# An opening on x^T laid out by the host, with the first two weight blocks in float32 for both token tiles

## The reference

```python
x = x + 0.5 * swiglu(rms_norm(x, ffn1_norm[l]), ffn1_wg[l], ffn1_wu[l], ffn1_wd[l])
x = x + hybrid_mixer(rms_norm(x, mix_norm[l]), positions, rel_bias, w_in[l], ...)
x = x + 0.5 * swiglu(rms_norm(x, ffn2_norm[l]), ffn2_wg[l], ffn2_wu[l], ffn2_wd[l])
```

## Time and profile before

| | us |
|---|---|
| median of 3 runs | 855.93 |
| the profiled execution | 856.22 |
| its span (first to last record) | 853.9 |
| TensorE busy | 846.0 |
| VectorE busy | 638.0 |
| ScalarE busy | 528.9 |

### The profile page before, as it was taken

How to read it: one execution, slowest core, us unless ns; L and a number is a source line. 1 busy time by engine, 2 the same in 40 slices (tenths; PEclk the granted TensorE clock), 3 DMA queues, 4 the chain that set the end, 5 groups by cost and what they waited for, 6 DMA issues and landing times.

```text
span 853.9 us, 11996 instructions
## 1 busy us (share of the span) xinstructions
PE 846.0 (99%) x4759; PEld 735.7 (86%) x4759; DVE 638.0 (75%) x809; ACT 528.9 (62%) x762; POOL 59.1 (7%) x65
## 2 busy tenths in 40 slices
PE   9999999999999999999999999999999999999997
PEld 8988888888889988888888887888888898888885
DVE  5999999987698656665466558858777777877873
ACT  6677777756575544653454356548676676776772
POOL 0022222310000000000000000100000001000001
PEclk9999999999999999999999999999999999999999
DMA  8976566554644655566546645577565664953501
GB/s 269 346 243 199 186 197 197 189 162 154 212 148 131 215 179 192 172 238 231 171 153 225 214 148 168 197 231 236 192 222 174 213 192 150 294 173 110 187 1 50
DMA packets 123847, 161.43 MB, mean 189 GB/s; under 512 B 3976, under 2 KB 111248, under 8 KB 123664
## 3 DMA queue, kind: packets, MB, share of 16 engines
q1 hardware_dynamic: 122176, 153.85, 54.9%
q0 software_dynamic: 1312, 6.29, 2.2%
q10 hardware_dynamic: 304, 0.53, 0.2%
HBM read 159.61 MB, written 1.05 MB: 188 GB/s over the span
## 4 chain that ended last, share of the span: by engine, by line
PE 97%; DVE 1%; ACT 1%; issue 0%; POOL 0%; POOLq 0%; DVEq 0%
PE pAcc L451 23%; PE pG L385 9%; PE pU L385 9%; PE pAcc L385 7%; PE pG L391 5%; PE pR L385 5%; PE pU L391 5%; PE pM L385 4%; PE pAcc L391 3%; PE pR L391 2%; PE pM L391 2%; PE pAcc L429 2%; PE pAcc L430 2%; PE pAcc L431 2%; PE pG L529 1%; PE pM L429 1%
## 5 line engine op out<-in xcount | busy, mean ns | idle before, releaser
L326 DVE TENSOR_TENSOR lo<-raw,hi 128x2048 fp32r<-128x2048 f32 x131 | 298.3, 2287 | 53.7 <-ACT hi L321 53.7
L321 ACT ACTIVATE hi<-raw 128x2048 fp32r<-128x2048 f32 x140 | 266.0, 1910 | 13.8 <-DMA raw<-in_ffn_wd 4.1
L385 PE MATMUL pG<-xT,hi 128*128 128x512 f32 x336 | 83.4, 390 | 0.0
L385 PE MATMUL pU<-xT,hi 128*128 128x512 f32 x320 | 80.0, 392 | 0.0
L451 PE MATMUL pAcc<-hi,h_hi 128*128 128x512 f32 x240 | 74.5, 392 | 0.0
L385 PEld LDWEIGHTS pG<-xT,hi 128*128 128x128 f32 x336 | 62.8, 188 | 13.6 <-issue 0.7
L451 PE MATMUL pAcc<-lo,h_hi 128*128 128x512 f32 x240 | 74.0, 389 | 0.0
L451 PE MATMUL pAcc<-hi,h_lo 128*128 128x512 f32 x240 | 73.9, 389 | 0.0
L1166 ACT ACTIVATE h_hi<-h 128x512 fp32r<-128x512 f32 x28 | 17.7, 633 | 80.3 <-PE pAcc L451 74.5
L385 PEld LDWEIGHTS pU<-xT,hi 128*128 128x128 f32 x320 | 58.0, 189 | 10.6
L1702 DVE TENSOR_TENSOR h_lo<-h,h_hi 128x512 fp32r<-128x512 f32 x28 | 19.2, 688 | 46.0 <-ACT h_hi L1166 45.9
(11 more groups left out here) (522 smaller groups left out, 1662.8 us busy)
## 6 DMA issues: line engine op xcount, KB each, us to landing
raw<-in_a_w_in SPq DMA_DIRECT2D x24, 1024.0 KB, 5.3
raw<-in_ffn_wd SPq DMA_DIRECT2D x22, 1024.0 KB, 5.6
raw<-in_ffn_wg SPq DMA_DIRECT2D x21, 1024.0 KB, 5.4
raw<-in_ffn_wu SPq DMA_DIRECT2D x21, 1024.0 KB, 6.2
raw<-in_w_in SPq DMA_DIRECT2D x16, 1024.0 KB, 5.5
raw<-in_a_w_out SPq DMA_DIRECT2D x8, 1024.0 KB, 5.1
raw<-in_w_kv SPq DMA_DIRECT2D x8, 1024.0 KB, 5.5
raw<-in_b_w_qz SPq DMA_DIRECT2D x8, 1024.0 KB, 5.4
```

What stands on the lines that cost most here:

```text
L321: act.activation(HI[n % NHL][:, :], RAW[n % NRAW][:, :], ACT.Copy).then_inc(S["hi"], 1)
L326: dve.tensor_tensor(LO[n % NHL][:, :], RAW[n % NRAW][:, :], HI[n % NHL][:, :].bitcast(f32), ALU.subtract).then_inc(S["lo"], 1)
L385: end = pe.matmul(v3(bank[:, :], 2), wh[:, k, w], x4[:, :, k, :], start=start and k == 0, stop=not start and k == KD - 1, skip_group_check ...
```

## The change

The host lays out x^T beside x: for each token tile, 128 features on the partitions, and 8 chunks of them by 128 tokens along the row. The kernel loads its four pieces on SyncE's queue, the first two ahead of block 0, the others behind it. The norm vector is alone and first on ScalarE's queue. No x is transposed; TensorE's list has six idle multiplies, the vector's transpose, three more idle multiplies, and then float32 products only: blocks 0 and 1 for both tiles. Block 1 is never split. Block 2 is split in halves instead (`hi_first`, `lo_first`).

The squares are now of x^T, so the sum over features is made in two steps: VectorE adds over the 8 chunks (`sum_first`), TensorE over the 128 partitions, by a product with a column of 1/1024 (`mean_square`). The rows of x, which the residual needs at the end of the first swiglu, are loaded later, by one DMA of 1 MB ahead of block 8's. Block 4's load waits until block 0 is multiplied, block 5's until block 1 is; before, both waited for block 0, and for the splits of blocks 0 and 1. The tensors for the bias are laid out by the host for all 128 partitions, in two loads instead of four, behind block 3.

```diff
         def load_block(sp, n):
-            if n >= NRAW:
+            if n in (NRAW, NRAW + 1):
+                sp.wait_ge(S["used"], n - NRAW + 1)
+            elif n > NRAW:
                 sp.wait_ge(S["lo"], n - NRAW + 1)
-            if n in (NRAW, NRAW + 1):
-                sp.wait_ge(S["used"], 1)
...
+        def load_x_t(engine, b):
+            c = slice(b * 512, (b + 1) * 512)
+            engine.dma_start(XRAW[:, c], T["x_t"][:, c]).then_inc(S[f"x_in{b}"], 16)
...
+        def load_x(sp):
+            sp.wait_ge(S["x_sum"], 2)
+            sp.dma_start(v3(X[:, :], NT), T["x"][0].rearrange("(t p) c -> p t c", p=P)).then_inc(S["x_rows"], 16)
...
+        def mean_square(pe, t):
+            pe.wait_ge(S["x_sum"], t + 1)
+            pe.matmul(VAR[t], SSQ[:, t * P:(t + 1) * P], MEAN, start=True, stop=True).then_inc(S["x_var"], 1)
+
         def pe_start(pe):
-            busy(pe, 7)
-            x_transposes(pe, 0, 0)
-            pe.wait_ge(S["gain0"], 16)
+            busy(pe, 6)
+            pe.wait_ge(S["gain_first"], 16)
             pe.transpose(ACC[1][:, 0:KD], G8, IDENT[0:KD, 0:KD]).then_inc(S["gc_ps"], 1)
-            x_transposes(pe, 0, 1)
+            busy(pe, 3)
             pe.wait_ge(S["xf0"], 1)
             pe.wait_ge(S["first0"], 16)
             first_block(pe, 0, G, 0, range(0, 4))
             pe.wait_ge(S["xf1"], 1)
             pe.wait_ge(full[0], LANDED[0])
-            first_block(pe, 0, G, 0, range(4, 6))
+            first_block(pe, 0, G, 0, range(4, KD))
+            mean_square(pe, 0)
+            pe.wait_ge(S["xf2"], 1)
+            first_block(pe, 0, G, 1, range(0, 4))
             power_row(pe, 0)
-            first_block(pe, 0, G, 0, range(6, KD))
-            x_transposes(pe, 1, 0)
-            x_transposes(pe, 1, 1)
+            pe.wait_ge(S["xf3"], 1)
+            first_block(pe, 0, G, 1, range(4, 6))
+            mean_square(pe, 1)
+            first_block(pe, 0, G, 1, range(6, KD)).then_inc(S["used"], 1)
             pe.wait_ge(S["first1"], 16)
-            first_block(pe, 1, U, 0, range(0, 4))
+            first_block(pe, 1, U, 0, range(0, 2))
             power_row(pe, 1)
+            first_block(pe, 1, U, 0, range(2, 4))
             pe.wait_ge(full[1], LANDED[1])
             first_block(pe, 1, U, 0, range(4, KD))
-            pe.wait_ge(S["xf2"], 1)
-            pe.wait_ge(S["xf3"], 1)
-            first_block(pe, 0, G, 1, range(0, KD)).then_inc(S["used"], 1)
-            pe.wait_ge(S["lo"], 2)
-            pe.wait_ge(S["xt_lo"], 3)
-            to_tokens(pe, 1, U, XT, (1,), half_way=4).then_inc(S["used"], 1)
+            first_block(pe, 1, U, 1, range(0, KD)).then_inc(S["used"], 1)
+            pe.wait_ge(S["xt_lo"], 4)
...
         def xt_first(dve, b):
-            dve.wait_ge(S["xt_ps"], b + 1)
-            dve.tensor_tensor(xf(b), v3(XBANK[b][:, :], 4), fbc(GC[:, 4 * (b % 2):4 * (b % 2) + 4], P),
+            dve.wait_ge(S[f"x_in{b}"], 16)
+            dve.tensor_tensor(xf(b), x_raw(b), fbc(GC[:, 4 * (b % 2):4 * (b % 2) + 4], P),
                               ALU.mult).then_inc(S[f"xf{b}"], 1)
+        def square_first(act, b):
+            act.wait_ge(S[f"x_in{b}"], 16)
+            half = slice(4 * (b % 2), 4 * (b % 2) + 4)
+            act.activation(squares(b // 2).rearrange("p c k -> p k c")[:, half, :], x_raw(b), ACT.Square).then_inc(S["ssq"], 1)
+
+        def sum_first(dve, t):
+            dve.wait_ge(S["ssq"], 2 * t + 2)
+            dve.tensor_reduce(SSQ[:, t * P:(t + 1) * P], squares(t), AX.X, ALU.add).then_inc(S["x_sum"], 1)
...
# VectorE, second factor of the first h
-                        dve.tensor_tensor(H[:, BC:512], U[:, BC:512], SA[:, BC:512], ALU.mult).then_inc(S["h"], 1)
+                        k = RS_COL["norm", 0, 1][0]
+                        dve.scalar_tensor_tensor(out=H[:, BC:512], in0=U[:, BC:512], scalar=ST[:, k:k + 1], in1=SA[:, BC:512],
+                                                 op0=ALU.mult, op1=ALU.mult).then_inc(S["h"], 1)
...
# SyncE
-            load_x(sp, 0, 0)
+            load_x_t(sp, 0)
+            load_x_t(sp, 1)
             load_half(sp, 0, 0)
             load_half(sp, 0, 1)
-            load_x(sp, 1, 0)
-            load_x(sp, 1, 1)
+            load_x_t(sp, 2)
+            load_x_t(sp, 3)
             load_half(sp, 1, 0)
             load_half(sp, 1, 1)
             load_block(sp, 2)
-            sp.dma_start(POS[:, 0:TOK], T["positions"][0].partition_broadcast(P),
-                         allow_slow_non_contiguous=True).then_inc(S["bias_pos"], 16)
...
             load_block(sp, 3)
+            sp.dma_start(POS[:, 0:TOK + NT], T["bias_positions"]).then_inc(S["bias_pos"], 16)
+            sp.dma_start(TABLES[:, 4 * NSTEP:], T["bias_tables"]).then_inc(S["bias_pos"], 16)
             for n in range(LEAD + 1, NB):
                 b = BLOCKS[n - LEAD]
-                if b == ("ffn1", "gate", 3):
+                if b == ("ffn1", "gate", 2):
+                    load_x(sp)
+                elif b == ("ffn1", "gate", 3):
...
# ScalarE
-            load_x(act, 0, 1)
             load_gain_first(act)
             act.wait_ge(S["half"], 1)
             warm(act, ACT.Square)
-            for t in range(NT):
-                for c in range(2):
-                    act.wait_ge(S[f"x_in{t}{c}"], 16)
-                    square(act, 0, t, c)
+            for b in range(4):
+                square_first(act, b)
+            warm(act, ACT.Silu)
             xt_hi_first(act, 0)
             xt_hi_first(act, 1)
-            hi_half(act, 0)
-            hi_half(act, 1)
-            warm(act, ACT.Silu)
             xt_hi_first(act, 2)
             xt_hi_first(act, 3)
-            hi(act, 2)
+            hi_first(act, 0)
+            hi_first(act, 1)
...
# VectorE
             xt_first(dve, 0)
             xt_first(dve, 1)
-            variance(dve, 0, 0)
+            sum_first(dve, 0)
+            xt_first(dve, 2)
+            xt_first(dve, 3)
+            variance_first(dve, 0)
+            sum_first(dve, 1)
             norm_first(dve, 0)
             norm_first(dve, 1)
-            variance(dve, 0, 1)
-            xt_first(dve, 2)
-            xt_first(dve, 3)
+            variance_first(dve, 1)
             xt_lo_first(dve, 0)
             xt_lo_first(dve, 1)
             norm_first(dve, 2)
             norm_first(dve, 3)
-            lo_of_half(dve, 0)
-            lo_of_half(dve, 1)
             xt_lo_first(dve, 2)
             xt_lo_first(dve, 3)
-            lo(dve, 2)
+            lo_first(dve, 0)
+            lo_first(dve, 1)
```

More of the change, by code:

```diff
@@ L57 @@
 NRAW, NHL = 4, 4
+UNSPLIT = 2
 LEAD = 3
@@ L100 @@
     "hi": "hi parts of weight blocks", "lo": "lo parts of weight blocks", "used": "weight blocks multiplied",
-    "x_in00": "x of token tile 0 loaded, its first half", "x_in01": "its second half",
-    "x_in10": "x of token tile 1 loaded, its first half", "x_in11": "its second half",
+    "x_in0": "x^T of token tile 0 loaded, its first half", "x_in1": "its second half",
+    "x_in2": "x^T of token tile 1 loaded, its first half", "x_in3": "its second half",
+    "x_sum": "squares of a token tile summed over the chunks of features",
+    "x_var": "and over the features of a chunk", "x_rows": "x loaded", "mean": "1 / D",
     "first0": "first half of weight block 0 loaded", "first1": "first half of weight block 1 loaded",
@@ L105 @@
     "xf2": "that of token tile 1, first half", "xf3": "its second half",
-    "gc_ps": "first gain by features in a bank", "gc": "and in SBUF", "rb": "powers of the first norm along columns",
-    "hi_first": "hi part of the first half of block 1",
+    "gain_first": "first gain loaded", "hi_first": "hi part of the first half of block 2", "gc_ps": "first gain by features in a bank", "gc": "and in SBUF", "rb": "powers of the first norm along columns",
     "const_in": "lambda vectors, subln gain and DFT matrices loaded",
@@ L296, in load_half, with hi_first, lo_first @@
                 full[n] if half else S[f"first{n}"], 16)
-        def hi_half(act, half):
-            act.wait_ge(*((full[1], LANDED[1]) if half else (S["first1"], 16)))
+        def hi_first(act, half):
+            if not half:
+                act.wait_ge(full[UNSPLIT], LANDED[UNSPLIT])
             c = slice(half * KD * BC // 2, (half + 1) * KD * BC // 2)
-            op = act.activation(HI[1][:, c], RAW[1][:, c], ACT.Copy)
-            if half:
[L305 to L314, removed]
+            op = act.activation(HI[UNSPLIT][:, c], RAW[UNSPLIT][:, c], ACT.Copy)
+            op.then_inc(*((S["hi"], UNSPLIT + 1) if half else (S["hi_first"], 1)))
+        def lo_first(dve, half):
+            dve.wait_ge(*((S["hi"], UNSPLIT + 1) if half else (S["hi_first"], 1)))
+            c = slice(half * KD * BC // 2, (half + 1) * KD * BC // 2)
+            op = dve.tensor_tensor(LO[UNSPLIT][:, c], RAW[UNSPLIT][:, c], HI[UNSPLIT][:, c].bitcast(f32), ALU.subtract)
+            if half:
+                op.then_inc(S["lo"], UNSPLIT + 1)
```

(25 more changed lines are left out.)

35 lines of the change are left out of this document (16 added, 19 removed).

## The result

The changed kernel takes 856.92 us (median of 22 runs, 855.96 to 860.09), the kernel before 855.92 (22 runs beside them, 855.41 to 856.27). The ratio is 1.0018, 95% interval 1.0012 to 1.0024. The forecast was 855.55, the range 854.7 to 856.5. By the medians the change makes the kernel slower by 1.0 us, by the means, which the highest times pull up, by 1.5 us (857.41 against 855.89). Its times scatter five times as far: 12 runs lie between 855.96 and 856.93 (the lower group), nine between 857.50 and 858.86 and one at 860.09 (the upper group). 0.2% would be 1.71 us; the ratio is just within it, its interval reaches beyond.

A forecast was written before the change was run, and what follows sets the result against it. TensorE was taken to bound the kernel. Start -0.94, low clock +0.43, transposes -0.88, block 1 +0.57 and feature sums +0.44 gave -0.38 us, so 855.93 became 855.55; range 854.7 to 856.5.

The forecast's parts named there:

- Which bound: Whole kernel: TensorE bounds it, busy 846.0 of 853.9 us; only shortening its list or starting it sooner gains time.
- The same bytes stand before it now, so I leave it there: Opening loads: block 0's first half still lands at 5.96 us, with 512 KB of x ahead of it.
- bound 6.44: Block 0's first-half landing: later bound, for one more DMA issued ahead on SyncE's queue, 0.48 us.
- Rival 3: Opening: weights or VectorE's chain to block 2 are the wait; 855.9 to 856.4 us; chance 0.18 shared with another rival.
- the prediction's own signs: Changed trace: wrong if start moves under 0.5, spacing halves before 6.5 or after 8.3, or TensorE waits between 21 and 60.
- The start at 6.04: First real product on TensorE: starts at 6.04 instead of 6.98 us, 0.94 gained, 0.5 at the worst bound.
- The level of the clock: TensorE's opening: clock still rises at about 7.4, so three records instead of one run low, 0.43 us lost.
- rival 2: TensorE's opening: a standstill delays the clock's rise, 0.213 us per further low record, up to 858.3 us; chance 0.12.
- The sums on TensorE: Two sums over features by one-column products: 0.22 us each, 0.44 for both, bounds 0.22 and 0.86.
- The chain to block 2: VectorE's work to block 2: last half ends at 20.5, needed at 21.35, so 0.85 us are left.
- The loads: Later weights and rows of x: block 4 issued at about 14, block 5 at 21.4; cost taken as nothing.
- The sum: Opening's TensorE total: -0.38 us, ending at 21.35, passed whole to the kernel's end.

The follow-up runs named there:

- f4_vec_late: Changed kernel with x^T's second piece moved to the head of ScalarE's queue, the norm vector behind it; median 855.26 us.
- e2_gap: Changed kernel without the three idle multiplies behind the norm vector's transpose; median 858.39 us.
- e0_after: The changed kernel run once more, with no edit; median 858.62 us.
- g2_late_gap: f4_vec_late without the three idle multiplies behind the norm vector's transpose; median 856.79 us.
- e1_fill: Changed kernel with six idle multiplies instead of three behind the norm vector's transpose; median 856.75 us.
- g4_weights_first: Changed kernel with block 0's first half first on SyncE's queue, x^T's first piece then the vector on ScalarE's, two idle multiplies behind the transpose; median 856.93 us.
- h2_best: f4_vec_late with four idle multiplies instead of three behind the norm vector's transpose; median 855.87 us.
- h1_vec_waits: Changed kernel with the norm vector's load issued only after x^T's first piece has landed, behind ScalarE's table load; median 861.70 us.

## Why the prediction was wrong

- **Which bound, and that the opening's end passes to the kernel's end whole:** right. The span less the opening's end is 832.2 to 832.3 in every trace.
- **"The same bytes stand before it now, so I leave it there" (block 0 at 5.96, bound 6.44):** this step failed. The measured landings are 6.92 to 8.1. The bytes are the same, but before, one of the pieces of x was issued on the second queue at the first moment, and I counted the move as 0.48 us of issue time only. With that piece back at the head of the second queue (f4_vec_late) the block lands at 5.76 and the median is 855.26. Rival 3 named the weights as the wait, but took the 6.44 of the bound for the worst landing. By the prediction's own signs, a start that moves by less than 0.5, it was wrong: the first product moved from 6.98 to 7.06.
- **The start at 6.04:** all but the weights was as said: vector transposed at 4.65, its copy started at 4.69, the first half of x^T multiplied by 5.5. The idle multiplies ended at 6.05.
- **The level of the clock, three low records, no gap in TensorE's work:** the gap was there, by the failed step. In e2_gap its cost is rival 2's, a late rise, with the place and the price per record named there (0.213): 3.0 us. In e0_after (1.6 us) it is another, which I hadn't named: the clock had risen and was put back. And I took the standstill as 0.44 at most and gave the rival 0.12; about half of the executions are of the upper group, by one or the other. The sentence of the Trainium skill on the rise (TensorE: Matmul & The Clock Gate, What's actually happening), that it comes at another point from run to run, is borne out: the first product ran wholly at the upper level in after, whereas before's first record ran low, and in two executions of the same kernel the last six idle records took 1.47 (after) and 0.94 (e0_after). I turned it down on three runs; 22 runs of before lie 0.86 us apart.
- **The sums on TensorE:** a sum over features took 0.12, not 0.22, but each group of products behind it took 0.1 more than priced. From the end of the first product to the end of the opening I had 11.05 (10.3 to 21.35), measured 11.03.
- **The chain to block 2:** forecast 20.5, measured 18.70 + 2.36 = 21.06, TensorE takes it at 21.4 to 21.8. It held, with no wait.
- **The loads:** block 4 was issued at 14.80, block 5 at 21.82; no TensorE wait is seen from 21.8 to 190.
- **The sum:** in the trace of after the end is 21.78 instead of 21.35: +1.02 for the start, -0.57 for the first product (3.69, at the upper level, for 4.26), -0.02 for the rest. In the median execution it is 1.0 us worse still; the traces show later landings and low records as what does that. Luck took something off the miss as well: I carried over the 2.32 us that the profiled execution took beyond its span, and after's took 1.96. Over all executions the medians are 1.94 and 2.2. Nothing here shows why. By the medians of the spans the change costs 1.3 us (855.0 against 853.7 for the kernel before beside the experiments), and f4_vec_late gains 0.5.

## What to carry to other kernels

A wait of TensorE in the opening can cost more than its length. With block 0 early in both, about 1 us of standstill while the clock was low (g2_late_gap) put the median 1.5 us above f4_vec_late's, and in the changed kernel half of the executions are in the upper group. Idle multiplies that run until the clock has risen took that away; whether they reach to the landing mattered less (e1_fill). In this kernel it paid to put a large load first on each of the two issuing queues, and the small one behind it. That isn't free of risk: the vector behind a piece of x^T was in time in f4_vec_late, but with the weights first on the other queue it landed only at 5.53 (g4_weights_first). And when one profile shows a landing that nothing waits for, don't take its time as the price of a step that will wait for it: one edit with that wait, repeated, shows the scatter that a single trace hides.

## What the runs showed of the hardware

- One issuing queue at the start: 176 to 305 GB/s in each microsecond from 3 to 6 us, against 336 to 388 with a 256 KB piece on a second queue from 0.74 (before, f4_vec_late, and the rest of g2_late_gap, g4_weights_first and h2_best, which each have one microsecond lower, 252 to 307).
- TensorE's clock fell to 0.50 in e0_after at the end of a standstill of 2.56 us, and the 5.29 us of the first product that followed ran largely at the lower level. In h1_vec_waits it fell near 8.0, in a standstill that began at 4.46. It stayed up through a standstill of 1.47 us in e1_fill. The windows write 1.00 for the low stretch ahead of the first rise, so there only the spacing of records tells the level.
- A float32 product with one moving column, 128x128 stationary, takes 0.12 us in the chain.
